# Moving the low parts of split operands to other addresses in SBUF

## The reference, cut to what matters

```python
for l in range(2):
    x = layernorm(ALPHA * x + 0.5 * swiglu(x, ffn1_in[l], ffn1_out[l]), ln1)
    qa, ka, va, zb, xbc, dtb, qc, kc, vc, gpre = split(x @ w_mix_in[l])
    o_a = diff_attention(qa, ka, va)      # branch 1
    o_b = mamba2(zb, xbc, dtb)            # branch 2
    o_c = stick_breaking(qc, kc, vc)      # branch 3
    proj = einsum('bsrc,rcd->bsrd', stack(o_a, o_b, o_c), w_branch[l])
    mix = einsum('bsrd,bsrd->bsd', sigmoid(gpre + gate_bias[l]), proj) @ w_mix_out[l]
    x = layernorm(ALPHA * x + mix, ln2)
    x = layernorm(ALPHA * x + 0.5 * swiglu(x, ffn2_in[l], ffn2_out[l]), ln3)
```

## Time and profile before

| | us |
|---|---|
| median of 3 runs | 1984.0 |
| lowest, highest | 1982.02, 1987.06 |
| the profiled execution | 1982.76 |
| its span, first to last instruction | 1981.0 |
| TensorE busy | 1958.2 |
| TensorE weight loads busy | 1796.0 |
| VectorE busy | 1395.6 |
| ScalarE busy | 1095.6 |
| GpSimd busy | 149.7 |

### The profile page before, as it was taken

How to read it: one execution, slowest core, us unless ns; L and a number is a source line. 1 busy time by engine, 2 the same in 40 slices (tenths; PEclk the granted TensorE clock), 3 DMA queues, 4 the chain that set the end, 5 groups by cost and what they waited for, 6 DMA issues and landing times.

```text
span 1981.0 us, 35361 instructions
## 1 busy us (share of the span) xinstructions
PE 1958.2 (99%) x14178; PEld 1796.0 (91%) x14178; DVE 1395.6 (70%) x2098; ACT 1095.6 (55%) x1761; POOL 149.7 (8%) x150
## 2 busy tenths in 40 slices
PE   8999999999999999999999999999999999999998
PEld 7889899899988889998999989998888989899996
DVE  7877688746566686778875656657678677886555
ACT  6687476534444577658544444444568756753442
POOL 1200000000000002710000000000000370000000
PEclk9999999999999999999999999999999999999999
DMA  8544467545745544643645755575454564464563
GB/s 283 164 136 136 165 196 235 197 131 195 262 161 170 170 139 150 203 157 130 226 148 192 254 170 163 195 259 175 149 170 129 166 197 149 150 213 149 191 213 126
DMA packets 272891, 354.71 MB, mean 179 GB/s; under 512 B 10211, under 2 KB 226045, under 8 KB 272765
## 3 DMA queue, kind: packets, MB, share of 16 engines
q1 hardware_dynamic: 271421, 348.71, 53.6%
q0 software_dynamic: 1344, 4.23, 0.8%
HBM read 351.83 MB, written 1.08 MB: 178 GB/s over the span
## 4 chain that ended last, share of the span: by engine, by line
PE 87%; DVE 6%; ACT 4%; issue 2%; DMA 1%; POOL 0%; SPq 0%; DVEq 0%; ACTq 0%
PE ps L809 24%; PE ps L811 16%; PE ps L818 16%; PE ps L819 7%; PE ps L813 7%; PE ps L803 3%; PE ps L804 3%; PE ps L805 3%; DVE ring_r L1973 2%; ACT ring_hi L1463 1%; PE ps L1338 1%; DVE tok_r L1973 1%; PE ps L1269 1%; PE ps L1061 1%; ACT tok L1895 1%
## 5 line engine op out<-in xcount | busy, mean ns | idle before, releaser
L1973 DVE TENSOR_TENSOR ring_r<-ring,ring_hi 128x1024 fp32r<-128x1024 f32 x602 | 732.2, 1225 | 386.8 <-ACT ring_hi L1463 384.8
L1463 ACT ACTIVATE ring_hi<-ring 128x1024 fp32r<-128x1024 f32 x602 | 631.8, 1059 | 561.4 <-PE ps L818 341.9
L809 PE MATMUL ps<-xT_hi,ring_hi 128*128 128x256 f32 x2784 | 665.2, 281 | 0.8 <-DVE xT_r L1973 0.8
L811 PE MATMUL ps<-xT_r,ring_hi 128*128 128x256 f32 x2784 | 654.9, 278 | 0.0
L809 PEld LDWEIGHTS ps<-xT_hi,ring_hi 128*128 128x128 f32 x2784 | 524.4, 188 | 16.4 <-issue 11.6
L811 PEld LDWEIGHTS ps<-xT_r,ring_hi 128*128 128x128 f32 x2784 | 524.7, 188 | 0.1
L818 PE MATMUL ps<-xT_hi,ring_r 128*128 128x256 f32 x2784 | 374.7, 277 | 0.0
L818 PEld LDWEIGHTS ps<-xT_hi,ring_r 128*128 128x128 f32 x2784 | 343.6, 188 | 0.0
L2747 POOL TENSOR_TENSOR small<-small,const 128x1 f32<-128x1 f32 (+3 forms) x32 | 39.7, 1241 | 1793.4 <-DVE small L2422 1237.8
L813 PE MATMUL ps<-ring_hi,tok_r 128*128 128x512 f32 x344 | 133.9, 389 | 0.0
L809 PE MATMUL ps<-ring_hi,xT_hi 128*128 128x512 f32 x328 | 130.8, 399 | 1.2 <-DVE tok_r L1973 0.9
(11 more groups left out here) (380 smaller groups left out, 2857.2 us busy)
## 6 DMA issues: line engine op xcount, KB each, us to landing
ring<-in_w_mix_in SPq DMA_DIRECT2D x88, 1024.0 KB, 5.2
ring<-in_ffn_w_in SPq DMA_DIRECT2D x80, 1024.0 KB, 5.1
ring<-in_ffn_w_out SPq DMA_DIRECT2D x44, 1024.0 KB, 4.9
ring<-in_w_branch SPq DMA_DIRECT2D x24, 1024.0 KB, 5.3
ring<-in_w_ffn_up SPq DMA_DIRECT2D x22, 1024.0 KB, 5.1
ring<-in_w_in SPq DMA_DIRECT2D x21, 1024.0 KB, 5.1
ring<-in_w_ffn_down SPq DMA_DIRECT2D x11, 1024.0 KB, 5.1
ring<-in_w_mix_out SPq DMA_DIRECT2D x8, 1024.0 KB, 6.0
```

Of the source, the lines that this page charges most:

```text
L809: pe.matmul(out_, stat[0], mov[0], start=first, stop=False)
L811: pe.matmul(out_, stat[0], mov[1], start=False, stop=False)
L1463: act.activation(half_of(high_of(s), s, q), half_of(ring[:, s % SLOTS, :], s, q), ACT.Copy).then_inc(w_hi, 1)
L1973: return dve.tensor_tensor(lo, whole, hi.bitcast(F32), ALU.subtract)
```

## The change

It alters declarations and views alone; the instructions, their order and their semaphores stay as they are.

- xT (low part xT_lo), qT and qcT are no longer tensors of their own. They become three neighbouring pieces of a new tensor `lows`, declared behind vc, starting 3 words (12 bytes) into it. xT_hi, kT and kcT, the high parts, stay tensors, and so do xbc and vc.
- tok grows by 64 words (256 bytes). zT, with its low part zT_lo, begins 51 words later in it than before, 3 words above a multiple of 16; mT stays where it was.
- With these the low parts of xT, qT, zT and qcT begin 12 bytes higher, counted by 256, than their high parts.

```diff
-        tok, tok_r = both("tok", [P, 3 * T * D])
+        tok, tok_r = both("tok", [P, 3 * T * D + 64])
         const, const_r = both("const", [P, CONST_W])
         sb("apart", [P, 8])
         x = sb("x", [P, T, D])
         xT_hi = sb("xT_hi", [P, KD, TOK], F32R)
-        xT, xT_lo = both("xT", [P, KD, TOK])
-        qT, qT_r = both("qT", [P, KD, TOK])
         kT, kT_r = both("kT", [P, KD, TOK])
         xbc, xbc_r = both("xbc", [P, N_XBC, TOK])
-        qcT, qcT_r = both("qcT", [P, KD, TOK])
         kcT, kcT_r = both("kcT", [P, KD, TOK])
         vc_, vc_r = both("vc", [P, T * D])
+        Z_AT = 51
+        LOW_AT = 3
+        lows, lows_r = both("lows", [P, 3 * KD * TOK + 8])
+        xT, qT, qcT = (lows[:, LOW_AT + i * KD * TOK:LOW_AT + (i + 1) * KD * TOK].rearrange("p (k n) -> p k n", n=TOK) for i in range(3))
+        xT_lo, qT_r, qcT_r = (lows_r[:, LOW_AT + i * KD * TOK:LOW_AT + (i + 1) * KD * TOK].rearrange("p (k n) -> p k n", n=TOK) for i in range(3))
...
-        tok1 = tok[:, :].rearrange("p (t n) -> p t n", t=T)
+        tok1 = tok[:, 0:3 * T * D].rearrange("p (t n) -> p t n", t=T)
...
-        mT, zT = (feats_of(tok[:, i * T * D:(i + 1) * T * D]) for i in (1, 2))
-        mT_lo, zT_lo = (feats_of(tok_r[:, i * T * D:(i + 1) * T * D]) for i in (1, 2))
+        mT, mT_lo = (feats_of(a[:, T * D:2 * T * D]) for a in (tok, tok_r))
+        zT, zT_lo = (feats_of(a[:, 2 * T * D + Z_AT:3 * T * D + Z_AT]) for a in (tok, tok_r))
```

## The result

The changed kernel takes 1997.9 us (median of 6 runs, 1997.1 to 1999.4), the kernel before 1985.1 (6 runs, 1982.0 to 1988.4): a ratio of 1.0062, 95% interval 1.0050 to 1.0075. It is **slower** by about 12 us; the forecast was 1976.2. The profiled execution has a span of 1996.2 us against 1981.0.

The account below looks back on a forecast made before the run. TensorE, busy 99%, was taken as the bound: number of matmuls times spacing. A gain of 11.7 us, less 3.0 for odd starts and 0.9 handed back, gave 7.8: from 1984.0 to 1976.2 us, range 1965 to 1996.

Parts of the forecast that it names:

- the choice between the ends: Matmul spacing overall: between 20.0 us gained and 13.9 us lost, it expected 11.7 us of excess gone before deductions.
- the prediction's lower end: Pairs on xT take the rhythm of the second branch's alternating pairs, 3 and 2 ns more: 13.9 us lost.
- (a): Features form on xT, 2784 matmuls a line: excess of 5.6, 2.8 and 5.6 us above the floor, sum 14.0 us.
- L818: -2.8 forecast: High tokens on low weights, features form on xT: the bad rhythm expected gone, 2.8 us gained.
- (b): Row form, xT stationary, 512 columns: 3.2 us of excess, half expected gone.
- (c): Staged blocks at 256 columns: 6.7 ns of excess each, 1.3 us in sum, half expected gone.
- (d): Second branch's product, high and low tokens on high weights: 1.5 us of excess, two thirds (1.0) expected gone.
- The tenth handed back: A tenth of the 8.7 us gain, 0.9 us, lost where TensorE would wait on VectorE and ScalarE instead.
- The odd start: Moving operands beginning inside a line: 3.0 us charged against the gain, with bounds of nothing and 20.4 us.
- Alternation costs: Rival, chance 0.15: pairs whose moving operands differ by 256 lose what the second branch loses, 13.9 us; time 1998.
- Its sign: Low tokens on high weights at a mean length of 280 ns or more all over would show that alternation costs.

Follow-up runs that it names:

- The sweep: Streams of 256-column matmuls alone on TensorE, moving operand at one constant start, 16-byte steps and some single words: 113.3 ns at 192 bytes, 120 one word above.
- (0,0): Stream of 24 matmuls alone on TensorE, every moving operand at 0 by 256 bytes, weights at 0: 120.0 ns spacing.
- (48,49): Stream of 24 matmuls alone on TensorE, moving operand alternating between 48 and 49 four-byte words by 64, weights at 0: 116.7 ns spacing.
- (48,51): Stream of 24 matmuls alone on TensorE, moving operand alternating between 48 and 51 four-byte words by 64, weights at 0: 116.7 ns spacing.
- (48,64): Stream of 24 matmuls alone on TensorE, moving operand alternating between 48 and 64 four-byte words, weights at 0: 116.7 ns spacing.
- the kernel that has none: The changed kernel with the high parts xT_hi, kT, xbc and kcT also moved by 12 bytes: 2018.7 us, ratio 1.0162.

## Why the prediction was wrong

**What held.** No new wait, no other engine and no DMA appeared; time is number times spacing, and spacing depends on addresses. That shifted tokens release the low-weight matmuls from the slow rhythm is true (74 to 30 halves), and so is that they fall to the floor within a few matmuls. VectorE's operations and the landings in the tile of qT added nothing that TensorE waited for: the layer norms' operations on it take 741 to 748 ns, and the slowest landing 7.4 us.

**The step that failed** is the choice between the ends: "With a shift of 12 bytes, not 192, I expect the bad rhythm gone in L818 (2.8 us), half of it gone in the xT pairs (5.6 of 11.2)". The pairs didn't lose half of the excess, they got a third rhythm of 116.7 ns, also in the 4 of 5 halves that had been on the floor. Forecast for them: -5.6 us; measured: +6.4 on the high tokens and +8.6 on the low ones (the first and third branches' low tokens in the latter), 15.0 in all, close to the 13.9 of the prediction's lower end. I had the row that says so: in the only alternating pairs of the trace, the second branch's, 14 spacings take 116.4 ns, and I had worked out 13.9 us from it. I set it aside because its difference was 192 bytes and this one 12, as if a small difference were nearly none. The sweep shows the opposite: one word above place 48 costs 6.7 ns, 256 bytes beside it cost nothing. The premise that a distance changing with each matmul can't hold a bad rhythm has fallen with it: alternation has steady rhythms of its own, 116.7 ns with 12 bytes and 120.0 with 16.

**The size of what could be won.** I summed (a) to 14.0 us from means rounded to whole ns, and charged L809, whose waits I could not clear, like L811. The spacings of the trace before give 2.6 (L809), 2.9 (L811) and 2.5 us (L818) above 113.3: 8.0 in all. Even a change that freed everything would have brought 8, not 14, in (a). Spacings between starts, counted only where nothing waits, are the number to sum; a mean length rounded to whole ns leaves 1.4 us open over 2784 matmuls.

**L818: -2.8 forecast.** Measured are -0.1 us with the starts behind waits and +0.6 without. 44 halves freed bring 44 x 8 x 4.4 = 1.5 us, but the first four of the eight pay 116 116 114 114 on their way down, 7 ns a half, 2.4 us over the 366 halves that aren't slow.

**(b), (c), (d): -2.3 and -1.0.** The row form came out +1.2 us in place of a gain: with xT_hi stationary, L821 went from 229.8 to 232.1 ns of spacing, L811 from 229.9 to 231.1, and L815 didn't move (229.3 and 229.4). The staged blocks did gain: kcT_r,xT_r from 119.6 to 117.7, kT_r,xT_hi from 121.1 to 117.4; 0.6 us in all at 256 columns. The earlier trace rows had them right as a place: both operands at 192 is relative 0, and (0,0) runs at 120.0 by itself. In the second branch 117.5 and 116.7 ns became 117.0 and 117.4: one alternation was traded for another, and nothing of the 1.0 came. The tenth handed back (0.9) was never tried, since there was no gain to hand back.

**The odd start: +3.0.** No run shows such a price: 16 bytes cost 36 us, 64 bytes what 12 bytes cost, and the streams (48,49), (48,51) and (48,64) all run at 116.7 ns, whether the second start is odd or round. The term was in the forecast without a cause; that a cost came at all is no merit of it.

**Rivals.** Alternation costs (0.15) gave 1998, and 1997.9 is what came, by the mechanism's place and price: L813 and L811 are past their old means, L820 is not. Its sign, L811 of old at 280 or more, was missed by 1 ns (279). Its reason is half right: that any difference by 256 costs the same has fallen with 16 bytes (120.0), and that there has to be a difference at all has fallen with the kernel that has none (2018.7). The Trainium skill ("SBUF — State Buffer", Who interferes with whom) lets PE wait on nobody; as far as other engines go, the program with TensorE alone agrees, since it shows paces from 113.3 to 120.0 ns without a neighbour. But one pace is not what follows from it.

**What stays open.** Why relative place 48 is good and its neighbours are not; what draws a stream of one layout into 113.3 or 117.7 (the lead does, but I found no rule); why place 51 alone runs at 116.6 in a program by itself and at 118 to 120 in the kernel. The runs show only that the pace is a property of the pair of starts, of their order, and of what went before.

## What to carry to other kernels

Before shifting a buffer that TensorE reads in a kernel bound by it, note where each moving operand begins relative to its stationary one by 256 bytes, and measure the pace of that pair in a small stream of matmuls; here a program of 24 matmuls per layout gave the kernel's 116.7 and 120.0 ns for the alternating pairs, but not the 118 to 120 ns of two operands at place 51, so it is a guide and not a proof. Keep the high and the low part at the same good place (here 192 bytes above the weights), shift only by multiples of 256 bytes, and don't argue that a small shift does little. What can be won is the sum of the spacings above the floor, here some 12 us over all matmuls of 256 columns, and should be read from starts, not from mean lengths.

## What the runs showed of the hardware

- A float32 matmul of this kind with 256 columns starts every 113.3 ns at best at the granted 2.4 GHz; by the operands' starts the settled spacing lies between that and 120.0, most often at 113.3, 116.7, 117.7, 118.3 or 120.0. A program in which no other engine works beside the streams shows all of these. With 512 columns: 226.6 to 236, and 243 at worst.
- As far as tried, the difference of the two operands' starts by 256 bytes counts, and not where both lie: +64 and +128 bytes on everything, or +256 and +512 on the low tokens, change nothing (0.9988 to 1.0005); +12, +16 and +64 bytes on the low tokens cost 0.6, 1.9 and 0.6%. This was tried with the high tokens at relative place 48 only.
- Two rhythms, 113.3 and 117.7 ns, are both stable at the same places. Kernels with the same relative places on xT showed 74, 78, 84, 89, 127, 129 and 131 slow halves of 396 in one trace each, with spans of 1981.0, 1982.0, 1981.1, 1982.1, 1983.2, 1984.2 and 1985.1 us. 101 ns a half is 5.8 us between the ends, where the spans differ by 4.1. 29 runs of the kernel before lay between 1981.0 and 1989.9 us, 0.45%: that the rhythm makes this scatter is likely, but there is only one trace of each kernel.
- With the first low tile of eight moved to relative place 32 or 64, all of 12 streams ended at 113.3 ns; moved to 56, 7 of 12 ended slow, behind the same leads as the 7 of the plain layout.
